# Reordering the mixer tails, the norm sums, the last dense down chunks and the first small loads of a two-block model kernel

## What is computed

```python
for l in range(DEPTH):                      # DEPTH = 2
    h = rms_norm(x, norm_mix[l])
    x = x + hybrid_mixer(h, ...)
    h = rms_norm(x, norm_ffn[l])
    x = x + (swiglu(h, ffn_wg, ffn_wu, ffn_wd) if l % 2 == 0 else moe_swiglu(h, ...))

def hybrid_mixer(h, ...):
    a, gate, u, v = split(h @ w_in)         # 512 columns each
    c = causal_depthwise_conv(a * sigmoid(gate), conv_w, conv_b)   # 31 taps
    c = silu(group_layer_norm(c, 8, conv_ng, conv_nb))
    v = group_layer_norm(gelu(v), 4, sgu_ng, sgu_nb)
    g_out = gelu(u) * (tril(sgu_w) @ v + sgu_b)                    # per chunk of 128 tokens
    return concatenate([c, g_out]) @ w_out
```

## Time and profile before

| | us |
|---|---|
| median of 3 runs | 1609.68 (1604.58 to 1610.06) |
| the profiled execution | 1611.48 |
| its span in the trace | 1609.7 |
| PE busy | 1529.3 (95%) |
| DVE busy | 1116.1 (69%) |
| ACT busy | 899.5 (56%) |

### The profile page before, as it was taken

How to read it: one execution, slowest core, us unless ns; L and a number is a source line. 1 busy time by engine, 2 the same in 40 slices (tenths; PEclk the granted TensorE clock), 3 DMA queues, 4 the chain that set the end, 5 groups by cost and what they waited for, 6 DMA issues and landing times.

```text
span 1609.7 us, 19484 instructions
## 1 busy us (share of the span) xinstructions
PE 1529.3 (95%) x7704; PEld 1289.2 (80%) x7704; DVE 1116.1 (69%) x980; ACT 899.5 (56%) x759; POOL 100.0 (6%) x110
## 2 busy tenths in 40 slices
PE   5988999979889999999999999999999599999997
PEld 5868999878688888888888888888887496777785
DVE  5966445359668888888888888888887543443555
ACT  4535434235437777676767777676775353343452
POOL 2600000026001000000000000000100200000000
PEclk9989999989979999999999999999999797998999
DMA  8437985344329999999999999999998442222250
GB/s 291 154 108 230 324 272 193 118 142 148 109 85 363 373 374 383 361 387 354 382 375 361 400 351 395 351 384 375 370 398 298 146 157 79 86 98 79 79 180 30
DMA packets 118955, 408.21 MB, mean 254 GB/s; under 512 B 5840, under 2 KB 31616, under 8 KB 118896
## 3 DMA queue, kind: packets, MB, share of 16 engines
q1 hardware_dynamic: 114576, 392.84, 66.8%
q0 software_dynamic: 3104, 10.22, 1.8%
q10 hardware_dynamic: 1216, 4.33, 0.7%
HBM read 400.02 MB, written 19.40 MB: 261 GB/s over the span
## 4 chain that ended last, share of the span: by engine, by line
PE 90%; DVE 4%; DMA 2%; ACT 2%; issue 1%; SPq 0%; POOL 0%; ACTq 0%; DVEq 0%; POOLq 0%
PE ps L460 24%; PE ps L461 24%; PE ps L462 24%; PE ps L2196 2%; PE ps L2407 1%; PE ps L2155 1%; PE ps L2156 1%; PE ps L2157 1%; DVE low L444 1%; DMA raw<-in_w_in 1%; PE ps L456 1%; DMA raw<-in_moe_wu 1%; PE ps L1214 1%; PE ps L1235 1%; PE ps L1201 1%
## 5 line engine op out<-in xcount | busy, mean ns | idle before, releaser
L450 DVE TENSOR_TENSOR low<-raw,high 128x2816 fp32r<-128x2816 f32 (+1 forms) x168 | 516.0, 3089 | 100.1 <-ACT high L439 100.0
L439 ACT ACTIVATE high<-raw 128x2816 fp32r<-128x2816 f32 (+1 forms) x168 | 428.3, 2560 | 103.3 <-PE ps L462 57.8
L460 PE MATMUL ps<-high,xTm_hi 128*128 128x512 f32 (+2 forms) x1152 | 427.0, 371 | 9.0 <-DVE xTm_lo L1776 4.1
L461 PE MATMUL ps<-low,xTm_hi 128*128 128x512 f32 (+2 forms) x1152 | 422.0, 366 | 0.0
L462 PE MATMUL ps<-high,xTm_lo 128*128 128x512 f32 (+2 forms) x1152 | 421.7, 366 | 0.0
L444 DVE TENSOR_TENSOR low<-raw,high 128x2816 fp32r<-128x2816 f32 (+2 forms) x72 | 203.3, 2828 | 84.0 <-ACT high L433 84.0
L460 PEld LDWEIGHTS ps<-high,xTm_hi 128*128 128x128 f32 x1152 | 217.5, 189 | 42.5 <-DVE xTm_lo L1776 4.6
L462 PEld LDWEIGHTS ps<-high,xTm_lo 128*128 128x128 f32 x1152 | 217.4, 189 | 28.3
L461 PEld LDWEIGHTS ps<-low,xTm_hi 128*128 128x128 f32 x1152 | 217.6, 189 | 27.9
L433 ACT ACTIVATE high<-raw 128x2816 fp32r<-128x2816 f32 (+2 forms) x72 | 168.5, 2343 | 111.8 <-PE ps L462 91.4
L460 PE MATMUL ps<-high,eT_hi 128*128 128x512 f32 x352 | 142.1, 404 | 0.0
(11 more groups left out here) (361 smaller groups left out, 1812.1 us busy)
## 6 DMA issues: line engine op xcount, KB each, us to landing
raw<-in_moe_wg SPq DMA_DIRECT2D x64, 1408.0 KB, 7.9
raw<-in_moe_wu SPq DMA_DIRECT2D x64, 1408.0 KB, 8.8
raw<-in_moe_wd SPq DMA_DIRECT2D x48, 1536.0 KB, 8.6
rawb<-in_w_in SPq DMA_DIRECT2D x25, 1024.0 KB, 5.2
raw<-in_w_in SPq DMA_DIRECT2D x16, 1024.0 KB, 5.3
raw<-in_moe_wd SPq DMA_DIRECT2D x16, 1024.0 KB, 8.4
raw<-in_ffn_wg SPq DMA_DIRECT2D x8, 1408.0 KB, 10.5
raw<-in_ffn_wu SPq DMA_DIRECT2D x8, 1408.0 KB, 10.5
```

The lines of the kernel that those rows point to most:

```text
L439: nc.scalar.activation(high[:, j % SPLITS, 0:n], raw[:, j % RAWS, 0:n], ACT.Copy).then_inc(hi_made, 1)
L450: nc.vector.tensor_tensor(low[:, j % SPLITS, 0:n], raw[:, j % RAWS, 0:n], f(high[:, j % SPLITS, 0:n]), ALU.subtract).then_inc(lo_made, 1)
L460: nc.tensor.matmul(out, xh, wh, start=first, stop=False)
L461: nc.tensor.matmul(out, xh, wl, start=False, stop=False)
```

## The change

Eight things move; nothing of the arithmetic is different, except that the sum of squares of block 1 comes from ACT in three of the norms.

- POOL waits until chunk 0 has landed before it issues its first small loads.
- In the norms n = 1, 2, 3 ACT takes block 1's sum of squares too (after block 0's high parts), and DVE's one is gone from `add_and_norm`.
- In the mixer tail ACT's first table load for the root stands ahead of the split of chunk 10 instead of in `group_norm(0)`, and the `high` of chunks 11 and 12 (in mixer 1: 47 and 48) each stand between the root and the silu, not after the silu.
- DVE does 12 solo taps, not 8, before it scales pair 0, the `low` of chunk 10 stands before that scaling, the solo sum before `conv_low(0)`, and the `low` of chunk 12 (48) before `group_scale(1)`.
- PE's `keep_warm(7, 8)` is gone and `keep_warm(2, 14)` is `keep_warm(2, 6)`; `spread(1)` moves from behind `out_chunk(2)` to its middle.
- The last two dense down chunks (34, 35) are taken block by block, and `acc_ready` comes after block 0's part of both.
- Chunk 37 (mixer 1's second) is no longer split inside the dense part.
- The split of the router's weights comes after the norm on both engines.

```diff
@@ -1461,6 +1461,7 @@
                     ins = pool.tensor_scalar(diag[:, k, :], ident, w, None, ALU.mult)
                 ins.then_inc(diag_made, 1)
 
+            pool.wait_ge(w_landed[0], 16)
             load_mix(0)
             pool.dma_start(croute[:, :], a["c_route"]).then_inc(route_landed, 16)
             pool.dma_start(router[:, :, :], a["moe_router"][0].rearrange("(t p) e -> p t e", p=P)).then_inc(route_landed, 16)
@@ -1516,8 +1517,10 @@
 
             def norm_std(n, b):
 
-                if b == 0:
-                    nc.scalar.activation(xn[:, 0, :], x[:, 0, :], ACT.Square, accum_out=sumsq[:, 0:1]).then_inc(sumsq_made[0], 1)
+                if b == 0 or n in (1, 2, 3):
+                    if b:
+                        act.wait_ge(x_made, 4 * n)
+                    nc.scalar.activation(xn[:, b, :], x[:, b, :], ACT.Square, accum_out=sumsq[:, b:b + 1]).then_inc(sumsq_made[b], 1)
                 act.wait_ge(sumsq_made[b], n + 1)
                 nc.scalar.activation(std[:, b:b + 1], sumsq[:, b:b + 1], ACT.Sqrt, bias=eps[:, 0:1], scale=1.0 / D).then_inc(std_made, 1)
 
@@ -1547,7 +1550,8 @@
                 def group_norm(m):
                     pair = slice(2 * m, 2 * m + 2)
                     centred, var = GN_BANKS[m]
-                    prepare(ACT.Sqrt)
+                    if m:
+                        prepare(ACT.Sqrt)
                     act.wait_ge(yc_filled, 2 * l + m + 1)
                     nc.scalar.activation(sq[:, pair, :], ps[:, centred, :].rearrange("p (t n) -> p t n", t=2),
                                          ACT.Square).then_inc(sq_made, 1)
@@ -1557,6 +1561,7 @@
                     act.wait_ge(rstd8_made, 2 * l + m)
                     nc.scalar.activation(std8[:, :], ps[0:8, var, 0:T], ACT.Sqrt, bias=eps[0:8, 0:1]).then_inc(std8_made, 1)
                     prepare(ACT.Silu)
+                    high_upto(c0 + 11 + m)
                     act.wait_ge(yn_made, 2 * l + m + 1)
                     for t in (2 * m, 2 * m + 1):
                         nc.scalar.activation(sq[:, t, :], yT[:, t, :], ACT.Silu, scale=cols[:, 8 + t:9 + t],
@@ -1608,7 +1614,6 @@
                     nc.scalar.activation(xT_hi[:, 4 + 2 * m:6 + 2 * m, :], ps[:, TP[m], :].rearrange("p (t n) -> p t n", t=2),
                                          ACT.Copy).then_inc(cat_hi, 1)
                 group_norm(0)
-                high_upto(c0 + 11)
                 group_norm(1)
 
             act.dma_start(xm[:, :], a["meta_tokens_2"]).then_inc(meta_landed, 16)
@@ -1645,17 +1650,17 @@
                                      ACT.Copy).then_inc(ht_hi, 1)
 
             for j in range(FFN_CHUNKS):
-                high_upto(c0 + min(j + 2, FFN_CHUNKS + 1))
+                high_upto(c0 + min(j + 2, FFN_CHUNKS))
                 if j < 16 and j % 2 == 0:
                     dense_silu(j // 2)
                 for m in DENSE_AFTER.get(j, ()):
                     dense_hidden_high(m)
 
-            act.wait_ge(route_landed, 32)
-            nc.scalar.activation(router_hi[:, :, :], router[:, :, :], ACT.Copy).then_inc(router_hi_made, 1)
             prepare(ACT.Sqrt)
             act.wait_ge(x_made, 6)
             norm(2, 2)
+            act.wait_ge(route_landed, 32)
+            nc.scalar.activation(router_hi[:, :, :], router[:, :, :], ACT.Copy).then_inc(router_hi_made, 1)
             mixer(1)
             high_upto(MOE0 + 1)
             prepare(ACT.Sqrt)
@@ -1792,8 +1797,6 @@
                 add_output(n, 0)
                 norm_apply(n + 1, xn, 0)
                 add_output(n, 1)
-                dve.wait_ge(x_made, 4 * n + 4)
-                norm_sum(n + 1)
                 xt_low(n + 1, 0)
                 norm_apply(n + 1, xn, 1)
                 low_upto((MIX_CHUNKS, LAYER_CHUNKS, MOE0)[n] + 1)
@@ -1925,18 +1928,17 @@
                     nc.vector.tensor_tensor(xT_lo[:, 4 + 2 * m:6 + 2 * m, :], ps[:, TP[m], :].rearrange("p (t n) -> p t n", t=2),
                                             f(xT_hi[:, 4 + 2 * m:6 + 2 * m, :]), ALU.subtract).then_inc(cat_lo, 1)
                 group_rstd(0)
-                solo_taps(12, 20)
+                solo_taps(12, 24)
+                low_upto(c0 + 10)
                 group_scale(0)
-                low_upto(c0 + 10)
-                solo_taps(20, 28)
+                solo_taps(24, TAPS)
+                solo_sum()
                 conv_low(0)
-                solo_taps(28, TAPS)
-                solo_sum()
                 low_upto(c0 + 11)
                 group_rstd(1)
+                low_upto(c0 + MIX_CHUNKS)
                 group_scale(1)
                 conv_low(1)
-                low_upto(c0 + MIX_CHUNKS)
 
             nc.vector.memset(eps[:, :], EPS).then_inc(eps_made, 1)
             nc.vector.memset(row_of[:, :, :], 0.0).then_inc(eo_landed, 16)
@@ -1958,7 +1960,7 @@
             c0 = MIX_CHUNKS
 
             for j in range(FFN_CHUNKS):
-                low_upto(c0 + min(j + 2, FFN_CHUNKS + 1))
+                low_upto(c0 + min(j + 2, FFN_CHUNKS))
                 if j < 16 and j % 2 == 1:
                     q = j // 2
                     for b in range(NB):
@@ -1970,9 +1972,9 @@
                     dve.wait_ge(ht_hi, m + 1)
                     nc.vector.tensor_tensor(hT_lo[:, 2 * m:2 * m + 2, :], ps[:, TP[m % 2], :].rearrange("p (t n) -> p t n", t=2),
                                             f(hT_hi[:, 2 * m:2 * m + 2, :]), ALU.subtract).then_inc(ht_lo, 1)
+            add_and_norm(1)
             dve.wait_ge(router_hi_made, 1)
             nc.vector.tensor_tensor(router_lo[:, :, :], router[:, :, :], f(router_hi[:, :, :]), ALU.subtract).then_inc(router_lo_made, 1)
-            add_and_norm(1)
 
             mixer(1)
             add_and_norm(2)
@@ -2220,6 +2222,18 @@
                     c = c0 + 8 + n
                     pe.wait_ge(lo_made, c + 1)
                     k = OUT_ROWS[n]
+                    if n == 2:
+                        for r in range(2):
+                            for b in range(NB):
+                                for half in range(2):
+                                    cols2 = slice(r * D + half * 512, r * D + half * 512 + 512)
+                                    mm = three(ps[:, DOWN[2 * b + half], :], xT_hi[:, k + r, b * P:b * P + P],
+                                               xT_lo[:, k + r, b * P:b * P + P], high[:, c % SPLITS, cols2], low[:, c % SPLITS, cols2],
+                                               False, False)
+                            if r == 0:
+                                spread(1)
+                        mm.then_inc(w_used, 1)
+                        return
                     mm = row_product(xT_hi, xT_lo, (k, k + 1), c % SPLITS, lambda b, half: DOWN[2 * b + half], NB,
                                      n == 0, n == 3, done=acc_ready if n == 3 else None)
                     mm.then_inc(w_used, 1)
@@ -2264,7 +2278,6 @@
                 pe.wait_ge(conv_step, CONV_STEPS * l + PAIR_STEPS)
                 centred(0)
                 variance(0)
-                keep_warm(7, 8)
                 pe.wait_ge(cat_lo, 4 * l + 2)
                 pe.wait_ge(y2_made, l + 1)
                 out_chunk(0)
@@ -2275,8 +2288,7 @@
                 variance(1)
                 pe.wait_ge(cat_lo, 4 * l + 3)
                 out_chunk(2)
-                spread(1)
-                keep_warm(2, 14)
+                keep_warm(2, 6)
                 pe.wait_ge(cat_lo, 4 * l + 4)
                 out_chunk(3)
 
@@ -2307,17 +2319,31 @@
                         mm = product(b)
                 mm.then_inc(w_used, 1)
                 dense_transposes(pe, j)
-            for d in range(8):
+            for d in range(6):
                 c = c0 + 16 + d
                 pe.wait_ge(lo_made, c + 1)
                 tiles = down_tiles(d)
                 pe.wait_ge(ht_lo, tiles[-1] // 2 + 1)
                 if d == 0:
                     pe.wait_ge(silu_made, 16)
-                mm = row_product(hT_hi, hT_lo, tiles, c % SPLITS, lambda b, half: DOWN[2 * b + half], NB, d == 0,
-                                 d == 7, done=acc_ready if d == 7 else None)
-                mm.then_inc(w_used, 1)
+                row_product(hT_hi, hT_lo, tiles, c % SPLITS, lambda b, half: DOWN[2 * b + half], NB, d == 0,
+                            False).then_inc(w_used, 1)
                 dense_transposes(pe, 16 + d)
+            pe.wait_ge(ht_lo, FT // 2)
+            for b in range(NB):
+                for d in (6, 7):
+                    c = c0 + 16 + d
+                    pe.wait_ge(lo_made, c + 1)
+                    wh, wl = (slot_view(r, c % SPLITS, len(down_tiles(d)), D) for r in (high, low))
+                    for n, t in enumerate(down_tiles(d)):
+                        for half in range(2):
+                            cols2 = slice(half * 512, half * 512 + 512)
+                            mm = three(ps[:, DOWN[2 * b + half], :], hT_hi[:, t, b * P:b * P + P], hT_lo[:, t, b * P:b * P + P],
```

(5 more changed lines are left out.)

## The result

| | before | after |
|---|---|---|
| median of 7 runs each, us | 1606.77 (1599.82 to 1610.06) | 1594.39 (1590.01 to 1600.45) |
| ratio, after to before | | 0.9931, 95% interval 0.9906 to 0.9957 |
| span of the profiled execution, us | 1609.7 | 1594.1 |

A forecast was written before the change was run, and what follows sets the result against it. PE was taken as the bound (90% of the chain), idle at the start, mixer tails and stage borders. The terms summed to -12.4 us: profiled 1611.48 to 1599.1, median 1597.3 us; forecast 1594 to 1600.5 (0.55), range 1589 to 1604.

The forecast's parts named there:

- Start: Start of mixer 0: holding POOL's loads starts `high` of chunk 0 at 13.6 instead of 16.77, 3.2 us gained.
- the chain named: At the start: `gain` 2 us sooner, then norm, transposes and high parts end at 13.5, later than chunk 0's landing.
- Tails: Mixer tails: out_chunk(3) starts 28.9 and 29.1 us behind centred(0), gaining 7.2 in mixer 0 and 4.4 in mixer 1.
- The early split of chunk 12: Mixer tail: DVE's low of chunk 12 ahead of pair 1's scale costs 3.7 us before out_chunk(3).
- ACT's table load: Mixer tail: the moved table load was counted at 1.5 us, as in the trace.
- the other price: Mixer tails: the Trainium skill's 2.66 us for a table switch with drain would gain 1.2 us more in each.
- Clock in the tails: 3.6 us of PE idle before out_chunk(3) brings half clock for 3 us: 1.5 us lost per mixer (0 to 3.4).
- Borders from a mixer: Borders n = 0 and 2: DVE's sum of squares no longer ahead of block 0's xt_low, 1.0 and 1.1 us gained.
- Border from dense: Dense to mixer 1: block 1's later norm and chunk 37's split delay the first product, 1.5 us lost.
- The sign that PE would be idle before both blocks' transposes: Profile sign at the dense border: PE idle before both transposes, and about 6 us before mixer 1's first product.
- The rival in which somebody waits for them: Smaller gain, chance 0.18: PE waits for POOL's held loads (start gives nothing) or clock costs more; gain 5 to 9 us.

The follow-up runs named there:

- b1_tables_after_gain: Changed kernel, but POOL's first small loads wait for `gain` instead of chunk 0; first product of mixer 0 at 18.44 us, against 18.30 in the changed kernel.
- a2_low12_late: Changed kernel, but DVE makes the low of chunk 12 (48) behind conv_low(1), not ahead of group_scale(1); ratio to the kernel before 0.9879.
- a4_warm34: Changed kernel with 34 warm transposes ahead of out_chunk(3) instead of 6; first expert product at 464.90 us, 3.3 us sooner than in the changed kernel.
- d2_dve_sums: Changed kernel with DVE's sum of squares of block 1 back at the two borders from a mixer; first dense product at 123.67 us, second at 130.23.
- d1_dense_as_before: Changed kernel with the dense part's end as before: last two down chunks each over both blocks, chunk 37 split inside the dense part; ratio to the kernel before 0.9928.
- a3_border: Changed kernel, dense to mixer 1 reordered: ACT's sums of squares before all high parts, DVE's low of chunk 37 behind block 1's low parts; ratio to before 0.9877.
- a1_tables_at_once: Changed kernel with POOL's small loads issued at once again, without waiting for chunk 0; first product at 20.99 us, ratio to the kernel before 0.9937.

## Why the prediction came out right

The total was right within the noise: 12.4 us forecast, 11.3 us at the first expert product. Point by point:

- **Start.** Forecast -3.2 at the first product, found -2.8; the chain named (norm, transposes, high parts, with chunk 0 no longer last) is the one that b1_tables_after_gain and the trace show. Its head was to be `gain`; in the trace block 1's sum of squares, held by x, ends beside `gain`'s landing, and the norm starts 1.8 us sooner instead of 2. At the end of centred(0) only 2.0 is left: the first products ran at half clock for longer (granted 0.52 from 17.0 to 24.1). I had taken the clock's cost there as unchanged. That is chance in part, since the same start lost up to 1.2 us less in other kernels. It makes 1.2 us less than forecast in all, and is the largest error with that of the clock in mixer 1's tail.
- **Tails.** out_chunk(3) was put at 28.9 and 29.1 us behind centred(0) and stood at 28.3 and 28.6. That is 0.6 and 0.5 us better. The early split of chunk 12 was priced at 3.7 us and took 3.3 in each mixer (a2_low12_late). ACT's table load was put at 1.5 us; PE's wait before variance(0) went from 1.87 to 0.69, 1.2 us, and the other price, 1.2 us more in each tail, did not come.
- **Clock in the tails.** 1.5 us in each was forecast, 1.4 and 2.7 came; the second is a mis-sized term, within the 0 to 3.4 that was given. That the idle stretch is the cause was an inference from two places; a4_warm34 and the kernels beside it show it for mixer 1. For mixer 0 the agreement is luck: five of seven kernels with the same idle stretch lost nothing there.
- **Borders from a mixer.** 1.0 and 1.1 us were forecast and 1.2 came at each (by the second product), but the step that gave them holds for the kernel before only. There the sum of squares stood in the way by 1.0 us; in the changed kernel it would not have (d2_dve_sums), since the residual add no longer stands behind chunk 12's split. Two changes each give the gain, and I had counted one. I had noted that the add comes sooner and had written it off because the warm transposes hide block 0's norm. It was not hidden for what DVE does after that.
- **Border from dense.** +1.5 was forecast and +1.5 found, with PE's idle stretches of 3.62 us before block 1's transposes and 6.15 before the first product. The sign that PE would be idle before both blocks' transposes failed for block 0, and the prediction's own working had none there. d1_dense_as_before confirms the loss. a3_border removed both causes at once, so their shares stay open.
- **The held loads.** The rival in which somebody waits for them did not come: released at 11.9 us, they delayed nobody. The Trainium skill's rule on issuing early ("DMA: Bandwidth & Descriptors", Rules for kernel authors) would have had them at once; a1_tables_at_once did that, and its first product came 2.7 us later.
- **The total.** Errors of both signs cancel: 1.2 us less than forecast at the start, 1.2 less from the clock in mixer 1, against 1.1 more in the two tails' waits and 0.3 more at the borders. That it came out within 1.1 us is partly luck.

## What to carry to other kernels

In a program with hand-written orders, a split or prefetch for the next stage should stand beneath the matmuls that are already released, not between a step and the one it releases. The same 3 us of DVE work cost 3.3 us ahead of the last scale and nothing behind it. Where a border is reworked, follow the second block's path to its end, since a gain at the first block is taken by whatever stands in front of PE. And look at the granted clock behind each idle stretch: here a wait of 3.1 us cost another 1.3 to 2.8 in mixer 1 in each of seven kernels.

## What the runs showed of the hardware

- An idle stretch of PE can cost twice. Behind 3.1 us of idle the same 24 matmuls took 7.1 to 8.6 us instead of 5.8 in mixer 1 in all seven kernels that had it, and in mixer 0 7.2 and 7.3 in two, 5.8 in five. Filled with transposes that nobody reads, they took 5.8 in both. So the loss belongs in a range and not in a sum, and one kernel at full clock proves little.
- With 1.47 MB less in front of them, x, gain and chunk 0 landed in time for a start 2.7 us sooner, although another queue carried those bytes. From 5 to 12 us the two kernels moved nearly the same, 335 and 349 GB/s; before, 1.23 of the 2.34 MB were POOL's, after, all 2.44 MB were SP's. The queues share what there is.
- Untouched code behind the change took between 1115.6 and 1131.4 us in thirteen profiled executions. Nearly all of that is the last stretch, the attention block: 354.2 to 368.2 us. Before, and b1_tables_after_gain:

```profile
1241.50:1609.70 368.20, 337.02 (x1683) 261.78 (x1682) 165.30 (x203) 150.95 (x220) 10.57 (x13) 0.91 0.31 102
1228.40:1582.60 354.20, 324.05 (x1685) 254.33 (x1683) 165.32 (x203) 150.98 (x220) 10.16 (x13) 0.95 0.32 106
```

DVE and ACT are busy for the same time, and PE's idle time differs by 1 us, but the same matmuls take 13 us less, at a granted clock of 0.95 instead of 0.91. So this noise is PE's clock. What sets the clock there is not shown. It makes single times of these kernels unfit for comparing changes of a few us.
